# Where the matmul operands begin in SBUF: every streamed operand at a multiple of 512 bytes, the second buffers of the split weights 16 bytes behind one

## The reference

```python
def _swiglu(h, w_gate, w_up, w_down):          # h 512x1024, gate and up 1024x2816, down 2816x1024
    return (jax.nn.silu(h @ w_gate) * (h @ w_up)) @ w_down

for layer in range(DEPTH):                      # DEPTH = 2
    x = x + 0.5 * _swiglu(_rmsnorm(x, ffn1_norm[layer]), ...)
    proj = _rmsnorm(x, mix_norm[layer]) @ w_in
    ...                                         # SSD and S5, or attention and pooling
    x = x + mixed @ w_out
    x = x + 0.5 * _swiglu(_rmsnorm(x, ffn2_norm[layer]), ...)
...
mix = hybrid_mixer(x, w_in_2, ...)              # 512x1024 @ 1024x7680 among others
x = layer_norm(alpha * x + mix); x = layer_norm(alpha * x + _swiglu(x, ...))
```

## The kernel before

| tensor | before | after |
|---|---|---|
| `X`, `Hh`, `Hl`, `raw0` to `raw3`, `wh0`, `wl0` | 128 | 0 |
| `wh1`, `wl1` | 128 | 16 |
| `RS`, `SS`, `ones` | 128 | 0 |
| `mats`, `M8` | 352 | 224 |
| `ffn_gh`, `ffn_gl`, `fin_gh/gl`, `even_mh/ml`, `odd_mh/ml`, `hybrid_mh/ml`, `OH`, `OL`, `CH`, `CL`, `QKV` | 480 | 0 |

## Time and profile before

### The profile page before, as it was taken

One profiled execution on the slowest core, in us unless ns is written; L12 is line 12 of the kernel. 1 busy time (PEld: TensorE's weight loads), 2 busy tenths in 40 slices (PEclk: granted clock), 3 DMA queues, 4 the chain that ended last, 5 costly groups with the idle time before them and its releaser, 6 DMA issues. The chain is left out here.

```text
span 2856.1 us, 33839 instructions
## 1 busy us (share of the span) xinstructions
PE 2746.2 (96%) x12804; PEld 2209.9 (77%) x12804; DVE 1445.4 (51%) x1853; ACT 962.2 (34%) x1320; POOL 224.9 (8%) x220
## 2 busy tenths in 40 slices
PE   8999999789999999999999999999999999799997
PEld 6878877568888888888767888888888787588885
DVE  5676247754443244432475544323898435633324
ACT  5433223443323233322244333222324542422312
POOL 2001014110000000000310000000000000300003
PEclk9999999999999999999999999999999999899998
DMA  4334334132223223232311232333541124122321
GB/s 154 118 122 149 117 117 141 47 118 96 95 95 109 86 88 99 96 106 88 112 52 48 95 100 96 110 107 106 145 134 60 45 64 143 59 95 95 109 93 49
DMA packets 77389, 282.69 MB, mean 99 GB/s; under 512 B 10208, under 2 KB 10848, under 8 KB 76400
## 3 DMA queue, kind: packets, MB, share of 16 engines
q1 hardware_dynamic: 66384, 248.49, 26.5%
q0 software_dynamic: 6304, 26.65, 2.9%
q10 hardware_dynamic: 4608, 6.30, 1.0%
HBM read 261.21 MB, written 13.89 MB: 96 GB/s over the span
## 5 line engine op out<-in xcount | busy, mean ns | idle before, releaser
L185 DVE TENSOR_TENSOR wl<-raw,wh 128x1024 fp32r<-128x1024 f32 (+2 forms) x440 | 566.3, 1287 | 1086.1 <-ACT wh L179 1085.3
L231 PE MATMUL PS<-Hh,wl 128*128 128x512 f32 x2160 | 846.2, 392 | 20.4 <-DVE wl L185 15.7
L233 PE MATMUL PS<-Hl,wh 128*128 128x512 f32 x2160 | 840.9, 389 | 0.0
L232 PE MATMUL PS<-Hh,wh 128*128 128x512 f32 x2160 | 840.6, 389 | 0.0
L179 ACT ACTIVATE wh<-raw 128x1024 fp32r<-128x1024 f32 (+2 forms) x440 | 480.2, 1092 | 1061.4 <-PE PS L233 901.2
L231 PEld LDWEIGHTS PS<-Hh,wl 128*128 128x128 f32 x2160 | 405.5, 188 | 118.6 <-issue 25.7
L233 PEld LDWEIGHTS PS<-Hl,wh 128*128 128x128 f32 x2160 | 405.4, 188 | 84.4
L232 PEld LDWEIGHTS PS<-Hh,wh 128*128 128x128 f32 x2160 | 405.6, 188 | 83.8 <-issue 1.0
L233 PE MATMUL PS<-ffn_gl,wh 128*128 128x512 f32 x880 | 351.1, 399 | 0.0
L232 PE MATMUL PS<-ffn_gh,wh 128*128 128x512 f32 x880 | 346.8, 394 | 0.0
L231 PE MATMUL PS<-ffn_gh,wl 128*128 128x512 f32 x880 | 345.4, 393 | 0.0
(11 more groups left out here) (471 smaller groups left out, 2604.3 us busy)
## 6 DMA issues: line engine op xcount, KB each, us to landing
raw<-in_gu SPq DMA_DIRECT2D x220, 512.0 KB, 3.4
raw<-in_dn SPq DMA_DIRECT2D x80, 704.0 KB, 4.0
raw<-in_hin SPq DMA_DIRECT2D x44, 512.0 KB, 3.5
raw<-in_oin SPq DMA_DIRECT2D x16, 512.0 KB, 3.5
raw<-in_hin_gate SPq DMA_DIRECT2D x16, 512.0 KB, 3.5
X<-QKV ACTq DMA_DIRECT2D x96, 64.0 KB, 2.0
kept_x<-X POOLq DMA_DIRECT2D x16, 256.0 KB, 3.6
raw<-in_eout SPq DMA_DIRECT2D x8, 512.0 KB, 4.6
```

Of the source, the lines that this page charges most:

```text
L185: self.nc.vector.tensor_sub(self.wl[j % SPLIT][:, 0:kw], self.raw[j][:, 0:kw], self.wh[j % SPLIT][:, 0:kw].bitcast(F32)).then_inc(self.lo_ ...
L231: self.nc.tensor.matmul(out, wl, xh[:, u.k0 + k, :], start=first, stop=False)
L232: self.nc.tensor.matmul(out, wh, xh[:, u.k0 + k, :], start=False, stop=False)
L233: done = self.nc.tensor.matmul(out, wh, xl[:, u.k0 + k, :], start=False, stop=last)
```

## The change

Nothing is computed otherwise and no instruction is added, removed or moved: the instruction streams of all engines are the same, operation by operation. What differs is where the tensors lie. A spacer `lead` of 384 bytes moves `X` and all behind it to a multiple of 512. `wh1` and `wl1` are allocated 512 bytes longer and used from their 16th byte on. A spacer `skew` of 160 bytes brings what is allocated stage by stage to a multiple of 512 again.

```diff
         self.stage_sems, self.retired, self.clearing = None, [], []
+        self.lead = self.sb("lead", [P, 96])
         self.X = self.sb("X", [P, DC, S])
         self.Hh = self.sb("Hh", [P, DC, S], F32R)
         self.Hl = self.sb("Hl", [P, DC, S], F32R)
         self.raw = [self.sb(f"raw{j}", [P, HALF * P]) for j in range(RAW)]
-        self.wh = [self.sb(f"wh{j}", [P, HALF * P], F32R) for j in range(SPLIT)]
-        self.wl = [self.sb(f"wl{j}", [P, HALF * P], F32R) for j in range(SPLIT)]
+        self.wh, self.wl = ([self.sb(f"{n}{j}", [P, HALF * P + P * j], F32R)[:, 4 * j:4 * j + HALF * P]
+                             for j in range(SPLIT)] for n in ("wh", "wl"))
...
         self.M8 = self.sb("M8", [P, S5G])
+        self.skew = self.sb("skew", [P, 40])
         self.PS = ctx.enter_context(nc.psum_tensor("PS", [P, 8, 512], F32))
```

## The result

The changed kernel took 2835.6 us (median of 4 runs, 2833.5 to 2837.0) against 2854.5 us before, a ratio of 0.9932 with a 95% interval of 0.9919 to 0.9945: 0.7% faster, 19 us. The prediction was 2832.6 us. The profiled execution spans 2834.7 us, 21.4 us less than the one of before.

The account below looks back on a forecast made before the run. TensorE's matmul count times start-to-start distance was taken as the bound. Down and output projections gain 21.8 us, other terms 0: span 2856.1 - 21.8 = 2834.3 us, median 2832.6 us; forecast's own range 2816 to 2849, all cases 2725 to 2872 us.

Parts of the forecast that it names:

- What bounds it: Whole kernel: TensorE, busy 96% of the span, hardly waits; time is the number of matmuls times their start-to-start distance.
- Down and output projections, 21.8 us: Their 3264 matmuls, streams moved from 480 to 0, take the up stages' pace, 6.67 ns less each: 21.8 us.
- Up projections, 0: Streams moved from 128 to 0: both operands move together, so no gain; at best 100 us.
- The 16 bytes, 0: 5388 matmuls with weights from `wh1`, `wl1`: offset small against the down stages' 352 bytes, so 0; break-even 4.0 ns.
- The sign of being right: Up stages keep 226.7 ns for even and odd `j` alike; down stages match, 443 matmuls per 100 us, not 430.
- Rival 2: The 16 bytes slow L231 to L233 in units with odd `j`, all stages: 2868.6 us, or 2878; chance 0.27.
- The sum: Profiled span: 2856.1 - 21.8 = 2834.3 us; as median of the runs, 2832.6 us.
- The way from span to time: Whole kernel: the median of the runs taken as 1.7 us lower than the profiled span.
- Both paces are steady: Up stages at 226.7 ns and down stages at 233.3 ns hold over 100 us stretches; neither is a wait.
- Two reads that get in each other's way: Split matmuls: the loss, 13.4 or 20.0 ns each, looks like interfering reads, not a property of the streamed operand alone.
- The argument from the read ports: TensorE's two independent read ports, by the skill, let weight loads take nothing from the stream; 16 bytes would cost nothing.
- The Trainium skill's pace: Full-clock matmuls start N / 2.4 GHz plus about 2.5 ns apart, 215.8 ns; if the change brought it, 2715 us.

Follow-up runs that it names:

- the aligned kernel: All tensors at a multiple of 512 bytes, without the change's 16-byte offset of `wh1` and `wl1`; 2839.3 us against 2857.2 before on that chip, ratio 0.9934.

## Why the prediction was right

*What bounds it:* right. Of the 21.4 us between the profiled spans, 18.6 are the pace of the split matmuls (26.6 to 8.0 us over 226.7 ns each); nothing on VectorE, ScalarE or the queues took its place. The rest is in the longer distances, 3.3 us shorter, which the prediction did not have, and 0.5 us the other way.

*Down and output projections, 21.8 us:* right in kind and in size. The alignment alone took 22.6 us off the pace (26.6 to 4.0), 1.0 of them in the `OH`/`OL` and `CH`/`CL` matmuls that were left out. The five down stages give 2640 matmuls by 6.67 ns, 17.6 us; the rest is the output projections, of which in the changed kernel the odd one came to a mean of 226.9 ns as counted and the even one, which is interrupted more often, only to 230.2.

*Up projections, 0:* right. The reason given, that both operands move together, was put to the test by having all at 480 (ratio 0.9931).

*The 16 bytes, 0:* near enough for the time, wrong as the reason was put. The step was "the offset is small against the 352 bytes of the down stages". Smallness has nothing to do with it: 8 bytes put a stage on the upper level, and these 16 bytes in all buffers cost 1.5% against the aligned kernel (1.0086 against 0.9934). In the changed kernel they cost 4.0 us of pace and not more because the units in between are at distance 0. The sign of being right, 226.7 ns in units with even and odd `j` alike, was met in unbroken stretches only. Rival 2 described a real price that this arrangement brings out in few places; its rule, units with odd `j` at 233.3 ns, holds for 18 of the 26 counted ones that start after other work.

*The sum:* that it is this close is in part luck. The pace went down by 22.6 - 4.0 = 18.6 us and the medians by 18.9, so the 3.0 us by which the time lies above the forecast are nearly the price of the 16 bytes. It stayed that small for a reason, the neighbours at distance 0, that the prediction does not have. The way from span to time compares unlike things, besides: an execution takes 1.7 to 1.9 us longer than its span in all that are on record, so the profiled execution before, with a span of 2856.1 us, took some 2857.8 us (an estimate from those), 3.4 us above the median and not 1.7. The forecast time stands all the same, as it is the median less 21.8 us. But the 21.4 us between the two profiled spans count 2.5 us more than the medians do.

*"Both paces are steady":* right, though one of the two "other down stages" is not another one: 290 to 390 us is the stage of the earlier trace rows.

*"Two reads that get in each other's way":* not borne out as it stood. Narrower loads lengthened the distance at 0 and shortened it by a quarter of the expected amount at 32 bytes, where that picture wanted it much shorter in both. What the runs show is weaker: where the four tensors stand alike modulo 256 bytes, the pace settles at 226.7 ns; where one of the weight tensors or both streamed ones stand apart, it is mostly 233.3, and at 16 bytes before the weights it is one or the other. What happens inside is open. The argument from the read ports against rival 2 is not borne out either: with the stream at 0, moving only the weights by 16 bytes put whole stages at 233.3 ns.

*The Trainium skill's pace*, 215.8 ns by "Wait — 56ns, not 53.3ns?" of TensorE: Matmul & The Clock Gate: no fp32r stretch of 512 columns in any run reached it; the lowest is 226.7.

## What to carry to other kernels

Where TensorE is busy throughout, read the distance from start to start and compare it between stages; a few per cent between stages with the same instruction shape point to where the tensors lie. Let streamed operands and weights of such fp32r streams begin at the same remainder modulo 256, by a spacer in the allocation; modulo 512 is the surer choice, since 256 bytes apart was seen in one stage only. Which remainder it is did not matter at 0, 128 and 480. Check it in the trace stage by stage: at 32 bytes apart, one weight tensor of the four tensors cost the whole sequence 3%, and 8 bytes did when both streamed tensors were moved.

## What was not expected of the hardware

- One and the same pair of addresses can hold two paces, 226.7 and 233.3 ns, for 120 us and longer, and which it is differs between stages of one run. It changed only at interruptions, in none of 36 unbroken sequences (all weights 16 bytes on; the kernel took 2866 to 2895 us).
- After an interruption a sequence at distance 0 takes some eight matmuls at about 231 ns to come back to 226.7.
- Loading 64 weight columns in place of 128 made the stream slower at distance 0, 230.0 for 226.7 ns, and faster at 32 bytes, 230.8 for 233.3.
- An fp32r matmul of 496 columns costs 220.0 ns, one of 480 only 3.3 ns less.
